# Gate and up products of two feed-forward layers: one 512-column product for the weights' high part, halves added on VectorE

## The reference, cut to what matters

```
def _swiglu(x, w_gate, w_up, w_down):
    return (jax.nn.silu(x @ w_gate) * (x @ w_up)) @ w_down

def second_block(x, ...):
    for i in range(DEPTH):          # DEPTH = 2
        h = ...                     # pooling in layer 0, attention in layer 1
        x = _layernorm(ALPHA_2 * x + h, ln_mix_g[i], ln_mix_b[i])
        x = _layernorm(ALPHA_2 * x + _swiglu(x, w_gate[i], w_up[i], w_down[i]), ln_ffn_g[i], ln_ffn_b[i])
    return x
```

## Time and profile before

| | |
|---|---|
| time, median of 3 runs | 1698.14 us (1696.96 to 1699.26) |
| the profiled execution: span from first to last instruction | 1695.9 us |
| PE busy | 1349.1 us, 80% of the span |
| PEld busy | 891.9 us, 53% |
| DVE busy | 604.9 us, 36% |
| ACT busy | 433.6 us, 26% |
| granted TensorE clock, mean over the span | 0.900 |
| steps of feed-forward layer 0 | 1188.24 to 1370.1 us |
| steps of feed-forward layer 1 | 1503.72 to 1685.9 us |

### The profile page before, as it was taken

How to read it: one execution, slowest core, us unless ns; L and a number is a source line. 1 busy time by engine, 2 the same in 40 slices (tenths; PEclk the granted TensorE clock), 3 DMA queues, 4 the chain that set the end, 5 groups by cost and what they waited for, 6 DMA issues and landing times.

```text
span 1695.9 us, 21317 instructions
## 1 busy us (share of the span) xinstructions
PE 1349.1 (80%) x8912; PEld 891.9 (53%) x8912; DVE 604.9 (36%) x1013; ACT 433.6 (26%) x704; POOL 41.5 (2%) x53
## 2 busy tenths in 40 slices
PE   9999565475475999993754647669999999999997
PEld 8785121121121675741211212126999979889996
DVE  5664000010000466630000000005655567875556
ACT  4552000000000433520000000004443455644443
POOL 2000000000000112000000000000000000000000
PEclk9999787797778999997877877789999999999999
DMA  9759999999999953699999999999555753065550
GB/s 364 219 217 400 432 430 429 431 427 433 429 431 427 394 185 124 277 403 427 432 430 430 429 429 432 429 426 391 186 169 195 247 198 114 13 240 172 197 197 25
DMA packets 130565, 536.82 MB, mean 317 GB/s; under 512 B 8148, under 2 KB 71892, under 8 KB 102716
## 3 DMA queue, kind: packets, MB, share of 16 engines
q1 hardware_dynamic: 126480, 530.08, 77.9%
q10 hardware_dynamic: 2380, 2.31, 0.9%
q0 software_dynamic: 1632, 3.38, 0.6%
HBM read 533.12 MB, written 2.62 MB: 316 GB/s over the span
## 4 chain that ended last, share of the span: by engine, by line
PE 53%; DMA 38%; DVE 5%; ACT 2%; SPq 2%; issue 1%; ACTq 0%; DVEq 0%
PE bank L2074 14%; PE bank L845 12%; DMA ring<-in_moe_w_down 11%; DMA ring<-in_moe_w_up 8%; PE bank L2092 7%; DMA arena<-in_moe_w_down 5%; DMA moe_slots<-in_moe_w_down 5%; PE bank L1389 5%; DMA xT_pair<-in_moe_w_up 5%; DMA moe_slots<-in_moe_w_up 4%; PE bank L1429 4%; PE bank L683 3%; PE bank L1723 1%; SPq L1639 1%; DVE stats L426 1%
## 5 line engine op out<-in xcount | busy, mean ns | idle before, releaser
L764 DVE TENSOR_TENSOR w_lo<-ring,w_hi 128x1024 fp32r<-128x1024 f32 x185 | 226.0, 1224 | 172.6 <-ACT w_hi L759 171.9
L1389 PE MATMUL bank<-ring,arena 128*32 128x512 f32 x960 | 218.2, 734 | 71.3 <-DMA arena<-in_moe_w_up 36.9
L759 ACT ACTIVATE w_hi<-ring 128x1024 fp32r<-128x1024 f32 x185 | 195.5, 1060 | 260.5 <-PE bank L2074 140.2
L1429 PE MATMUL bank<-ring,arena 128*32 128x512 f32 x496 | 146.1, 725 | 55.2 <-DMA ring<-in_moe_w_down 23.1
L2074 PE MATMUL bank<-xT_hi,w_lo 128*128 128x256 f32 x656 | 185.6, 283 | 0.0
L2074 PE MATMUL bank<-xT_lo,w_hi 128*128 128x256 f32 x656 | 185.6, 283 | 0.0
L2074 PE MATMUL bank<-xT_hi,w_hi 128*128 128x256 f32 x656 | 185.6, 283 | 0.0
L1553 DVE TENSOR_TENSOR arena<-arena,bank 64x512 f32<-64x512 f32 x32 | 22.1, 691 | 405.4 <-ACT arena L1490 405.4
L1389 PE MATMUL bank<-moe_slots,arena 128*32 128x512 f32 x352 | 109.4, 781 | 60.3 <-DMA ring<-in_moe_w_up 35.6
L1389 PEld LDWEIGHTS bank<-ring,arena 128*32 128x32 f32 x960 | 50.7, 130 | 154.9 <-issue 145.7
L1490 ACT ACTIVATE arena<-bank 64x512 f32<-64x512 f32 x32 | 18.8, 588 | 425.8 <-PE bank L1389 425.8
(11 more groups left out here) (334 smaller groups left out, 2427.3 us busy)
## 6 DMA issues: line engine op xcount, KB each, us to landing
ring<-in_moe_w_up SPq DMA_DIRECT2D x24, 2048.0 KB, 38.6
ring<-in_moe_w_down SPq DMA_DIRECT2D x22, 2048.0 KB, 40.0
ring<-in_moe_w_gate SPq DMA_DIRECT2D x20, 2048.0 KB, 39.8
moe_slots<-in_moe_w_gate SPq DMA_DIRECT2D x18, 2048.0 KB, 37.6
arena<-in_moe_w_up SPq DMA_DIRECT2D x14, 2048.0 KB, 37.9
arena<-in_moe_w_gate SPq DMA_DIRECT2D x12, 2048.0 KB, 38.7
ring<-in_w_gate SPq DMA_DIRECT2D x22, 1024.0 KB, 5.1
ring<-in_w_up SPq DMA_DIRECT2D x22, 1024.0 KB, 5.2
```

The source lines that it names most:

```text
L759: nc.scalar.activation(dst, raw, ACT.Copy).then_inc(hi_ready, 1)
L764: nc.vector.tensor_tensor(lo, raw, hi.bitcast(F32), ALU.subtract).then_inc(split_ready, 1)
L1389: last = nc.tensor.matmul(ps[B_GU[j % 2]][32 * c:32 * c + 32, :], xin[:, j, k, :], w, start=(k == 0), stop=(k == KD - 1), tile_position=(0 ...
L1429: last = nc.tensor.matmul(ps[B_DN[c]][32 * j:32 * j + 32, :], hT[:, j // 2, at:at + CAP], slot_row(ud[j], f % 2)[:, c * HALF:(c + 1) * HAL ...
```

## The change

x's two parts now lie in one tensor, `xT_parts`, so that one matmul can take the high and the low slice as 512 moving columns. In a gate or up chunk each slice is now one 512-column matmul of the weights' high part (x high into the bank's left half, x low into the right), and one 256-column matmul of the weights' low part with x high, into the right half. Gate and up of a block so take a bank each, four banks per step, and every step uses the same four. The wanted value is the sum of the bank's two halves. VectorE forms it with a `tensor_reduce` over pairs (512 elements in, 256 out): for gate in `gate_sum`, into SBUF, from where ScalarE now takes silu; for up in `product`, ahead of the multiplication. TensorE waits for the products of the step before (`fprod_ready`) ahead of a block's gate chunk. The first block has the same matmuls in another order, its second chunk shifted by two slices. The last block's hidden values are no longer formed at the end of the layer but in the last step. One load of the early part counts on another semaphore (`par_in` in place of `table_in`).

```diff
-        with nc.sbuf_tensor("xT_hi", [P, KD * SEQ], F32R) as xT_hi, nc.sbuf_tensor("xT_lo", [P, KD * SEQ], F32R) as xT_lo, \
+        with nc.sbuf_tensor("xT_parts", [P, 2 * KD * SEQ], F32R) as xT_parts, \
...
-            pe.wait_ge(table_in, 16)
...
+        def gate_up_bank(f, n):
+            return ps[2 * f + n]
...
+        def both_halves(f, n):
+            return gate_up_bank(f, n)[:, :].rearrange("p (h t) -> p t h", h=2)
...
-                for k in range(KD):
-                    if k % 2 == 0:
-                        pe.wait_ge(xhi_vec, n_x + k // 2 + 1)
-                    for wp, n in ((0, 0), (1, 0), (0, 1)) + ((1, 1),) * (m == 0):
-                        part(n, k, wp, xT_hi3, start=(k == wp == n == 0))
+                for k in range(KD + 2):
+                    if k < KD:
+                        if k % 2 == 0:
+                            pe.wait_ge(xhi_vec, n_x + k // 2 + 1)
+                        for wp in range(2):
+                            part(0, k, wp, xT_hi3, start=(k == wp == 0))
+                    if k >= 2:
+                        for wp in range(2 if m == 0 else 1):
+                            part(1, k - 2, wp, xT_hi3, start=(k == 2 and wp == 0))
...
                 for f in blocks:
+                    if before is not None:
+                        pe.wait_ge(fprod_ready, before + f)
                     for n in range(2):
                         pe.wait_ge(split_ready, at + (2 * f + n + 1))
...
                         for k in range(KD):
-                            for p, (wp, xp) in enumerate(PARTS):
-                                last = nc.tensor.matmul(ps[2 * s + f][:, n * SEQ:(n + 1) * SEQ],
-                                                        w[wp][:, k * P:(k + 1) * P],
-                                                        (xT_hi3, xT_lo3)[xp][:, k, :],
-                                                        start=(k == 0 and p == 0), stop=(k == KD - 1 and p == 2))
...
+                            both = nc.tensor.matmul(gate_up_bank(f, n)[:, :], w[0][:, k * P:(k + 1) * P], xT_both[:, :, k, :],
+                                                    start=(k == 0), stop=False)
...
+                            last = nc.tensor.matmul(gate_up_half(f, n, 1), w[1][:, k * P:(k + 1) * P], xT_hi3[:, k, :],
+                                                    start=False, stop=(k == KD - 1))
...
-                act.wait_ge(chunk_done, done)
-                nc.scalar.activation(f_silu[:, b, :], ps[b][:, 0:SEQ], ACT.Silu).then_inc(fsilu_ready, 1)
+                act.wait_ge(fgate_ready, blocks + 1)
+                nc.scalar.activation(f_silu[:, b, :], f_silu[:, b, :], ACT.Silu).then_inc(fsilu_ready, 1)
...
+            def gate_sum(s, f, done):
+                dve.wait_ge(chunk_done, done)
+                nc.vector.tensor_reduce(f_silu[:, 2 * s + f, :], both_halves(f, 0), AX.X, ALU.add).then_inc(fgate_ready, 1)
+
+            def product(s, f, blocks, done):
                 b = 2 * s + f
+                dve.wait_ge(chunk_done, done)
+                nc.vector.tensor_reduce(f_up[:, f, :], both_halves(f, 1), AX.X, ALU.add).then_inc(fparts_ready, 1)
+                dve.wait_ge(fparts_ready, 2 * blocks + 1)
                 dve.wait_ge(fsilu_ready, blocks + 1)
-                nc.vector.tensor_tensor(f_silu[:, b, :], f_silu[:, b, :], ps[b][:, SEQ:2 * SEQ], ALU.mult).then_inc(fprod_ready, 1)
+                nc.vector.tensor_tensor(f_silu[:, b, :], f_silu[:, b, :], f_up[:, f, :], ALU.mult).then_inc(fprod_ready, 1)
```

More of the change, by code:

```diff
@@ L2040, in gate_up_first, with part @@
                 n_x = split_before("x", gen)
[L2042 to L2043 removed]
+                def part(n, k, wp, x, low=False, start=False, stop=False):
+                    return nc.tensor.matmul(gate_up_half(0, n, int(low or wp)), w_parts[wp][:, n, k * P:(k + 1) * P],
                                             x[:, k, :], start=start, stop=stop)
@@ L2058, in gate_up_first @@
                             pe.wait_ge(xlo_ready, n_x + k // 2 + 1)
-                        last = part(n, k, 0, xT_lo3, stop=(n == 1 and k == KD - 1 and m == 0))
+                        last = part(n, k, 0, xT_lo3, low=True, stop=(k == KD - 1 and (n == 0 or m == 0)))
                     if n and m:
@@ new lines, in steps @@
+            def steps(g, first_step=False):
+                for s in range(2):
+                    at, blocks = g * 12 + (c0 + 4 + 6 * s), g * 4 + (m * NF + 2 * s + 2)
+                    us, ud = body[3 * s:3 * s + 2], body[3 * s + 2]
+                    split_hi(act, us[0], g, gate_up_chunk(us, 0, 0), 0, at)
+                    if first_step and s == 0:
+                        silu(0, 1, m * NF + 1)
+                    split_hi(act, us[1], g, gate_up_chunk(us, 0, 1), 1, at + 1)
+                    split_hi(act, us[0], g, gate_up_chunk(us, 1, 0), 0, at + 2)
+                    silu(1 - s, 0, blocks)
+                    split_hi(act, us[1], g, gate_up_chunk(us, 1, 1), 1, at + 3)
+                    split_hi(act, ud, g, down_chunk(ud, 0), 0, at + 4)
+                    silu(1 - s, 1, blocks + 1)
+                    split_hi(act, ud, g, down_chunk(ud, 1), 1, at + 5)
@@ L2141, in ffn_scalar @@
+            steps(0, True)
+            with act.Fori(1, 5) as g:
+                steps(g)
             for f in range(2):
                 split_hi(act, last_u, 0, down_chunk(last_u, f), f, c0 + FFN_CHUNKS - 2 + f)
-                if f == 0:
-                    silu(0, 1, c0 + FFN_CHUNKS - 4)
         def ffn_vector(dve, link, m, gen):
@@ L2167, in steps @@
                     split_lo(dve, gate_up_chunk(us, 0, 0), 0, at)
-                    for tile in todo[:1]:
-                        seed(dve, link, gen - 1, *tile)
+                    if now:
+                        parts(0, 0, m * NF)
+                        seed(dve, link, gen - 1, 0, 1)
                     split_lo(dve, gate_up_chunk(us, 0, 1), 1, at + 1)
-                    hidden(s, 1, blocks)
+                    if now:
+                        product(0, 1, m * NF + 1, c0 + 4)
+                        parts(0, 1, m * NF + 1)
@@ L2178, in steps @@
-                    for tile in todo[2:]:
-                        seed(dve, link, gen - 1, *tile)
-                    split_lo(dve, down_chunk(body[3 * s + 2], 1), 1, at + 5)
+                    product(1 - s, 0, blocks, at + 2)
+                    parts(1 - s, 0, blocks)
+                    split_lo(dve, down_chunk(ud, 0), 0, at + 4)
+                    gate_sum(1 - s, 1, at + 3)
+                    if now:
+                        seed(dve, link, gen - 1, 1, 1)
+                    split_lo(dve, down_chunk(ud, 1), 1, at + 5)
@@ L2182, in ffn_vector @@
+                    product(1 - s, 1, blocks + 1, at + 4)
+                    parts(1 - s, 1, blocks + 1)
             split_lo(dve, gate_up_chunk(first, 1, 0), 2, c0 + 2)
```

76 lines of the change are left out of this document (34 added, 42 removed).

## The result

The changed kernel takes 1721.62 us, median of 4 runs (1720.57 to 1721.79), against 1698.41 for the kernel before in the same session: a ratio of 1.0138 with the interval [1.0124, 1.0151]. It is slower by 1.4%. The forecast was 1716.5 us, with a range of 1703 to 1737. The profiled execution has a span of 1719.5 us, against 1695.9.

The account below looks back on a forecast made before the run. TensorE was taken to bound both feed-forward layers, with little slack in the weights' split chain. 16.7 + 1.4 - 0.4 + 0.7 = +18.4 us on 1695.9 gave 1714.3, plus 2.2 to the median: 1716.5 us, range 1703 to 1737.

Parts of the forecast that it names:

- TensorE's own step, 16.70: In each six-chunk step of the feed-forward layers, TensorE's own work falls from 17.11 to 16.70 us, 0.41 less.
- The new instructions: Per block on VectorE and ScalarE: each sum takes 0.69 us, the product 0.42, silu 0.42.
- The walk: One step followed through three engines' in-order queues: 1.24 us of TensorE waits, so 17.94 us instead of 17.11.
- The four waits: TensorE loses 0.40, 0.18, 0.49 and 0.17 us ahead of chunks 3, 4, 5 and the next chunk 0.
- the longer two ahead of chunks 3 and 5: Sign in the changed profile: of TensorE's four waits per step, those ahead of chunks 3 and 5 are longer.
- First step and first block: Each layer's first step costs 0.7 us more than a later one, twice 1.4; the first blocks' shifted matmuls add 0.7.
- The sum: Over the profiled span of 1695.9 us: 16.7 + 1.4 - 0.4 + 0.7 = +18.4 us, giving 1714.3.
- Priced at nothing: No cost for the wait on products, the moved semaphore, the four banks, the clock and the weights' transfers.
- Cheap sums: Rival: each VectorE sum takes 0.42 us, the step 16.97, the whole 1696.8 us, no change; chance 0.05.
- Faster: Rival: sums and silu fit idle time without moving high or low parts; 1690 us; chance 0.08.
- Nothing saved on TensorE: Rival: x's two stretches in one operand cost what the joined product saves; 1719 us, within the forecast's 0.72.
- has almost none: The split chain from chunk boundary to low part takes 2.52 us of a 2.88 us chunk, leaving 0.36 us.

Follow-up runs that it names:

- the last experiment: Against the kernel with sums and product ahead of the low parts (1694.4 us): 512-column product split back into two of 256 columns, sums kept; 1701.12 us, ratio 1.0018.
- TensorE's part alone: Changed kernel without the sums: silu and product read one half of their bank, so the result is incomplete; 1691.13 us, ratio 0.9964.
- the kernel with sums and product first: Changed kernel with VectorE's gate sums, up sums and products moved ahead of the low parts, only the splits of hidden values behind; 1694.41 us, ratio 0.9983.

## Why the prediction was right

It called slower, by the mechanism that was then found, and came out 5 us low. Its steps in its own order:

*TensorE's own step, 16.70.* The saving of 0.41 per step is nearly confirmed by the last experiment, 0.38 on average. In the changed kernel itself it is not had in full: most gate and up chunks there are 2.83 us without any wait, not 2.78, and a chunk that begins after a wait takes 0.11 more, as its second matmul comes 0.34 behind the first instead of 0.23.

*The new instructions.* Sum 0.684 against 0.69, product 0.426 against 0.42, silu 0.417 against 0.42. Priced by what it reads, the reduce was right; neither its 256 results nor the bank cost extra.

*The walk.* Starts of TensorE's chunks in us from chunk 0 of a step, the step of the rows above:

| start of | walk | measured |
|---|---|---|
| chunk 1 | 2.78 | 2.92 |
| chunk 3 | 8.74 | 8.76 |
| chunk 4 | 11.70 | 11.83 |
| chunk 5 | 14.98 | 15.14 |
| next chunk 0 | 17.94 | 18.34 |

The places of the waits and the order of the chain are right. The walk's step of 17.94 is 0.27 below the mean of 18.21 in layer 0, and 0.23 below the 18.17 of layer 1. This is the term that was mis-sized. The span came out 5.2 us above the forecast's 1714.3, and the nine steady steps of each layer make 2.4 and 2.1 us of that. (20 x 0.83 is also 16.6 and not the 16.7 of the sum, which changes nothing.)

The rows tell the pieces. Chunk 0 is 0.14 longer than counted (2.92). From low part to matmul I counted 0.17 and it is 0.05 (1293.62 + 1.23 to 1294.90): 0.12 too much. These two cancel, so it is luck that the start of chunk 3 is right to 0.02. The product starts 0.13 behind the up sum (1294.76 + 0.68 to 1295.57), where I counted 0.04, twice in a step. And where the loop turns, VectorE's next low part comes late: 0.09 behind the last split (1302.36, 1302.69 and 1303.20 in VectorE's time line), where inside the loop body it comes 0.08 ahead of its end. That is 0.17. In the step of the table it makes 0.14 - 0.12 + 0.18 + 0.17 = 0.37, against 18.34 - 17.94 = 0.40. The loop turns only three times in a layer, though, and costs about 0.06 a time in layer 1, so in the mean the pieces make 0.24 of the 0.27 and 0.20 of the 0.23.

*The four waits* have other sizes than I gave. Measured by how much further apart than usual the matmuls at a chunk's start stand, they are 0.18, 0.19, 0.45 and 0.18 us ahead of chunks 3, 4, 5 and 0 (0.37 for the last where the loop turns); the walk had 0.40, 0.18, 0.49 and 0.17. So the sign "the longer two ahead of chunks 3 and 5" came true for chunk 5 alone. Chunk 3 starts when I said, at 8.76, but TensorE comes to it only at 2.92 + 2 x 2.83 = 8.58, not at 8.34: its own longer chunks fill the first half of that wait.

*First step and first block.* The first step takes 18.47 in layer 0, the walk had 17.94 + 0.68 = 18.62. The first block, from its first matmul to chunk 2, takes 7.25 us instead of 6.76: +0.49, as counted (four matmuls of 0.12).

*The sum.* Layer 0 is 11.7 us longer and layer 1 11.1; predicted were 9.2 each. The remaining 0.8 us of the 23.6 arise ahead of layer 0, whose first matmul starts at 1181.94 instead of 1181.13. In the eight kernels of the experiments, which have the same early part, it starts between 1180.48 and 1181.61. So the 0.8 us look like scatter and not like the price of the moved semaphore.

*The clock* stayed at 1.00 in the new gaps, as the row by stretch shows.

*Priced at nothing.* The new wait on the products held: no weight load in the two layers is released by a product.

*The rivals.* Cheap sums: the reduce has the size that the forecast took, but halved it gave the time priced here within 2 us. Faster: its price of 1690 is what TensorE's part alone showed (1691.1), and its mechanism, silu's place, was the right one to name: with silu behind the high part the kernel is within 0.15% of before. The rival fell on its own condition, a sum plus silu of 0.65 us against 1.10. Nothing saved on TensorE: excluded by the last experiment (7 us).

One step of the reasoning was too gloomy, though it was not asked for a number: that the chain "has almost none" of slack. It has 0.36 us behind a high part, but the time in which ScalarE makes the high part is free for VectorE. The up sum and product (1.1 us) fit in there, the run of sum, product and splits (1.9 us) does not.

## What to carry to other kernels

When work is added to engines that are 40 to 60% idle, walk the queues in order around the instruction that the bounding engine waits for. What counts is what is queued ahead of it, and whether something ahead of it waits for a third engine. Here the same instructions in another order gave 1722, 1706, 1700, 1694 and 1692 us, so before a change is dropped as slower, put what the bounding engine waits for first, and the new work into the time in which that is still being made ready elsewhere.

## What the runs showed of the hardware beyond that

A gate/up chunk without any wait takes either 2.77 or 2.83 us, and often keeps to one of them for many chunks. In the kernel with sums and product first, the weight loads of one chunk of each kind, at a granted clock of 1.00:

```profile
1218.23 0.19 PEld L2092 LDWEIGHTS bank<-xT_parts,w_hi 128*128 128x128 f32 x1
1218.35 0.19 PEld L2096 LDWEIGHTS bank<-xT_parts,w_lo 128*128 128x128 f32 x1
1218.59 0.19 PEld L2092 LDWEIGHTS bank<-xT_parts,w_hi 128*128 128x128 f32 x1
...
1232.20 0.19 PEld L2092 LDWEIGHTS bank<-xT_parts,w_hi 128*128 128x128 f32 x1
1232.32 0.19 PEld L2096 LDWEIGHTS bank<-xT_parts,w_lo 128*128 128x128 f32 x1
1232.55 0.19 PEld L2092 LDWEIGHTS bank<-xT_parts,w_hi 128*128 128x128 f32 x1
```

The pairs stand 0.36 and 0.35 us apart. The lengths of before, 24 matmuls of 256 columns, were 2.88 throughout, and so were they in the kernel with the product taken apart. Changes of length fall on waits and on the starts of steps, but not on each; the strides of x are not the cause. Why a chunk takes the longer one stays open. It is worth up to 0.2 us in a step, 4 us in all.

A hand-over on VectorE from a sum to the product that needs it takes 0.03 to 0.04 us in the first pass, whose semaphore counts are constants, and 0.12 to 0.13 in the loop, where they are worked out from the loop's counter. All eight kernels that have the sums show it, but for one hand-over of 0.22 in the kernel with half sums. What in the loop costs it was not tried by itself.
